# Second halves of the forgetting group's values and of the output weights moved behind the next step's minima

## The reference

```python
u = rmsnorm(h, g_attn)
qa, ka, va, logf, qb, kb, vb = project(u, w_in, b_forget)
oa = fox_prompt(qa, ka, va, logf)     # 8 heads x 64, causal, bias sum of log forget
ob = swa_prompt(qb, kb, vb, rel_bias, sinks)   # window of 3 chunks of 64, with sinks
...
# fox: s = q k^T * scale + (c_q - c_k); p = softmax(s); o = p v
# the rows ka, va, logf are outputs too (fox_k, fox_v, fox_logf)
mixed = concat([rmsnorm(oa, g_out_a), rmsnorm(ob, g_out_b)])
h = h + mixed @ w_out
u = rmsnorm(h, g_ffn)
h = h + (silu(u @ w_gate) * (u @ w_up)) @ w_down
y = rmsnorm(h, g_final)
```

## Time and profile before

| | |
|---|---|
| Median of 3 runs | 1428.67 us (1427.84 to 1430.19) |
| The profiled execution's own time | 1427.94 us |
| Its span in the profile | 1426.1 us |
| TensorE busy | 1387.8 us, 97% of the span |
| VectorE, ScalarE, GpSimd busy | 576.9, 481.4, 213.4 us |
| Forgetting steps | from about 216 to 560 us |

### The profile page before, as it was taken

How to read it: one execution, slowest core, us unless ns; L and a number is a source line. 1 busy time by engine, 2 the same in 40 slices (tenths; PEclk the granted TensorE clock), 3 DMA queues, 4 the chain that set the end, 5 groups by cost and what they waited for, 6 DMA issues and landing times.

```text
span 1426.1 us, 22599 instructions
## 1 busy us (share of the span) xinstructions
PE 1387.8 (97%) x9041; PEld 1287.2 (90%) x9041; DVE 576.9 (40%) x1378; ACT 481.4 (34%) x1049; POOL 213.4 (15%) x317
## 2 busy tenths in 40 slices
PE   6999999999999899999999999999999999999997
PEld 5989898788888677889999999999999999999997
DVE  6345634242323433662343424242525252525156
ACT  6346555655554652553212121212121111121103
POOL 3145551634443330000000000000000000000000
PEclk9999999999999899999999999999999999999999
DMA  7621124212120444314202020202020202020003
GB/s 199 116 69 38 32 73 158 84 43 80 52 82 16 149 163 150 106 45 123 74 16 75 15 74 16 74 15 75 16 74 16 74 20 72 26 76 16 16 1 122
DMA packets 110256, 97.64 MB, mean 68 GB/s; under 512 B 15937, under 2 KB 96929, under 8 KB 109641
## 3 DMA queue, kind: packets, MB, share of 16 engines
q1 hardware_dynamic: 110152, 96.20, 23.2%
HBM read 77.07 MB, written 19.21 MB: 68 GB/s over the span
## 4 chain that ended last, share of the span: by engine, by line
PE 90%; DVE 3%; DMA 3%; ACT 2%; issue 2%; POOL 1%; SPq 0%; ACTq 0%; DVEq 0%
PE ps L602 28%; PE ps L603 26%; PE ps L604 26%; PE ps L806 2%; PE ps L736 1%; PE ps L953 1%; DMA cb<-c_scratch 1%; DMA ob<-o_scratch 1%; PE ps L818 1%; PE ps L683 1%; DVE ps L1645 1%; PE ps L897 1%; PE ps L774 1%; ACT sp_x L1276 0%; PE ps L701 0%
## 5 line engine op out<-in xcount | busy, mean ns | idle before, releaser
L1892 DVE TENSOR_TENSOR outs<-outs,ps 128x384 f32<-128x384 f32 (+1 forms) x264 | 134.4, 509 | 108.1 <-PE ps L604 107.8
L1878 DVE TENSOR_TENSOR gu<-ps,sg 128x384 f32<-128x384 f32 (+1 forms) x66 | 34.6, 524 | 237.6 <-PE ps L604 237.6
L2062 POOL TENSOR_TENSOR pl_x<-sp_x,ph_x 128x512 fp32r<-128x512 f32 (+5 forms) x120 | 102.2, 865 | 168.0 <-ACT sp_x L1276 166.7
L1456 ACT ACTIVATE h_hi<-gu 128x384 fp32r<-128x384 f32 (+1 forms) x66 | 32.9, 498 | 222.2 <-DVE gu L1878 222.2
L1275 ACT ACTIVATE ph_x<-ps,negc 128x512 fp32r<-128x512 f32 (+5 forms) x120 | 62.9, 524 | 83.6 <-PE ps L818 83.6
L1450 ACT ACTIVATE sg<-ps 128x384 f32<-128x384 f32 (+1 forms) x66 | 30.4, 465 | 171.7 <-PE ps L604 171.7
L602 PE MATMUL ps<-f_hi,ff0hi 128*128 128x384 f32 (+1 forms) x264 | 85.7, 325 | 0.0
L602 PE MATMUL ps<-f_hi,ff1hi 128*128 128x384 f32 (+1 forms) x264 | 85.6, 324 | 0.0
L602 PE MATMUL ps<-f_hi,ff2hi 128*128 128x384 f32 (+1 forms) x264 | 85.6, 324 | 0.0
L602 PE MATMUL ps<-f_hi,ff3hi 128*128 128x384 f32 (+1 forms) x264 | 85.6, 324 | 0.0
L603 PE MATMUL ps<-f_lo,ff0hi 128*128 128x384 f32 (+1 forms) x264 | 85.3, 323 | 0.0
(11 more groups left out here) (311 smaller groups left out, 3770.8 us busy)
## 6 DMA issues: line engine op xcount, KB each, us to landing
raw<-in_w_gate SPq DMA_DIRECT2D x22, 512.0 KB, 4.7
raw<-in_w_up SPq DMA_DIRECT2D x22, 512.0 KB, 4.8
raw<-in_w_down SPq DMA_DIRECT2D x22, 512.0 KB, 3.9
raw<-in_w_in SPq DMA_DIRECT2D x14, 512.0 KB, 4.1
cb<-c_scratch SPq DMA_DIRECT2D x4, 1312.0 KB, 7.2
xt<-in_x_prompt SPq DMA_DIRECT2D x8, 512.0 KB, 4.2
out<-outb SPq DMA_DIRECT2D x16, 256.0 KB, 2.9
ob<-o_scratch SPq DMA_DIRECT2D x16, 256.0 KB, 3.1
```

The lines of the kernel that those rows point to most:

```text
L1456: act.activation(h_hi[par][:, f, c0:c0 + n], gu[(f + c) % 2][:, 0:n], ACT.Copy).then_inc(S["g_hi"], 1)
L1878: dve.tensor_tensor(gu[(f + c) % 2][:, 0:n], bank(3 + c, n), sg[c][:, 0:n], ALU.mult)\
L1892: add = dve.tensor_tensor(y, y, bank(b, whole * P).rearrange("p (t m) -> p t m", t=whole), ALU.add)
L2062: pool.tensor_tensor(pl_x[at][0:rows, 0:n], sp_x[at][0:rows, 0:n], ph_x[at][0:rows, 0:n].bitcast(F32), ALU.subtract).then_inc(S["x_pl"], 1)
```

## The change

Three things are moved; no instruction is added or left out.

1. On ScalarE the first halves `vw_hi` (L1222, L1221) leave the task. The copy to `outb` stays where it was; the first halves now stand behind `fox_exp` of the step after the copy (pieces in part 3) or of the same step (the piece in part 0).
2. On VectorE, for every v, the second halves `vw_lo` stand behind the minima of that step.
3. On VectorE the second halves of the output weights leave the end of step v and stand behind the minima of step v + 1.

New semaphores `v_hi` and `v_lo` count the values' halves; the store of the rows waits for the copy alone (`fv_out`).

```diff
@@ ScalarE
                     out.then_inc(S["fv_out"], 1)
-                    act.wait_ge(S["fv_out"], rows_out(n))
-                    if i >= 1:
-                        act.wait_ge(S["x_pv"], 2 * (NFU * (i - 1) + {0: 8, 4: 12, 8: NFU}[t0]))
...
-                    act.activation(vw_hi[0:m, t0:t0 + count, 0:3:2, :], kept.rearrange("p n (h d) -> p n h d", h=2),
-                                   ACT.Copy).then_inc(S["ev_act"], 1)
+            def values_hi(*place):
+
+                for item, a in plan(*place):
+                    if item == "task" and TASKS[a[0]][0] == "fv":
...
+                        rows = outb[STORES.index(n) % 2][0:m, 0:count, :]
+                        act.activation(vw_hi[0:m, t0:t0 + count, 0:3:2, :], rows.rearrange("p n (h d) -> p n h d", h=2),
+                                       ACT.Copy).then_inc(S["v_hi"], 1)
...
                 if 0 <= v < NX:
                     fox_exp(v)
+                values_hi("x", v - 1, 3)
+                values_hi("x", v, 0)
@@ VectorE
             for v in range(-LEAD, NX + 2):
-                if v < 0:
...
-                else:
-                    if v == 0:
-                        values_lo(-1, 3)
-                    for part in range(5):
-                        items("x", v, part)
+
+                if v >= 0:
+                    items("x", v, 0, but="fv")
+                items("x", v, 1)
+                out_weights_lo(v - 1)
+                values_lo(v - 1, 3)
+                values_lo(v, 0)
+                for part in (2, 3, 4):
+                    items("x", v, part, but="fv")
                 if v == ROOT_AT:
                     roots_b()
-                for k in range(KB):
-                    if OUT_AT[k] == v:
-                        dve.wait_ge(S["cw_hi"], SPLIT_OUT + k + 1)
...
@@ SyncE
-                sp_.wait_ge(S["ev_act"], act_done(n))
+                if kind == "fv":
+                    sp_.wait_ge(S["fv_out"], rows_out(n))
+                else:
+                    sp_.wait_ge(S["ev_act"], act_done(n))
```

More of the change, by code:

```diff
@@ L304 @@
 LAST_LEAD = max(_item[1] for _item, _banks in HELD if _banks[0] > 1)
[L306 to L307 removed]
+BY_ACT = ("sk", "ck", "sv", "bias", "amw", "amx", "fk", "fc", "tb")
+BY_DVE = ("ck", "sv", "negc", "otw", "otx", "fc", "tb")
 def act_done(n):
@@ L1160, in task @@
                 b = 4 + BANK_OF["task", n]
-                if kind not in BY_ACT:
+                if kind not in BY_ACT and kind != "fv":
                     return
@@ L1212, in task @@
                     out.then_inc(S["fv_out"], 1)
[L1213 to L1223 removed]
+            def values_hi(*place):
+                for item, a in plan(*place):
+                    if item == "task" and TASKS[a[0]][0] == "fv":
+                        n = a[0]
+                        i, t0, count = TASKS[n][1]
+                        m = rows_of(t0)
+                        if i >= 1:
+                            act.wait_ge(S["x_pv"], 2 * (NFU * (i - 1) + {0: 8, 4: 12, 8: NFU}[t0]))
+                        elif t0 == 0:
+                            act.wait_ge(S["w_pv"], 2 * NWU)
+                            act.wait_ge(S["w_ttr"], 4 * NWU)
+                        if t0 == 8:
+                            act.wait_ge(S["cv_in"], 16 * (i + 1))
+                            act.activation(vw_hi[:, 9:11, 0:3:2, :], cache_v[:].rearrange("p n (h d) -> p n h d", h=2), ACT.Copy)
+                        act.wait_ge(S["fv_out"], rows_out(n))
+                        rows = outb[STORES.index(n) % 2][0:m, 0:count, :]
+                        act.activation(vw_hi[0:m, t0:t0 + count, 0:3:2, :], rows.rearrange("p n (h d) -> p n h d", h=2),
+                                       ACT.Copy).then_inc(S["v_hi"], 1)
             def items(*place):
@@ L1581, in task @@
                                       rows.rearrange("p n (h d) -> p n h d", h=2),
-                                      hi[0:m, t0:t0 + count, 0:3:2, :].bitcast(F32), ALU.subtract).then_inc(S["ev_dve"], 1)
+                                      hi[0:m, t0:t0 + count, 0:3:2, :].bitcast(F32), ALU.subtract).then_inc(S["ev_dve" if kind == "sv" else "v_lo"], 1)
                 elif kind == "tb":
@@ L1706, in values_lo, with out_weights_lo @@
                         task(*a)
+            def out_weights_lo(v):
+                for k in range(KB):
+                    if OUT_AT[k] == v:
+                        dve.wait_ge(S["cw_hi"], SPLIT_OUT + k + 1)
+                        dve.scalar_tensor_tensor(out=wo_lo[:, k, :], in0=raw2d[k % 3], scalar=gw_col[:, OUT_K[k]:OUT_K[k] + 1],
+                                                 in1=wo_hi[:, k, :].bitcast(F32), op0=ALU.mult, op1=ALU.subtract)\
+                           .then_inc(S["cw_lo"], 1)
             def items(*place, but=None):
```

23 lines of the change are left out of this document (8 added, 15 removed).

## The result

The kernel with the change took 1438.61 us (median of 4 runs, 1435.29 to 1439.76), the kernel before, run beside it, 1428.79 us (4 runs, 1427.84 to 1430.19). The ratio is 1.0064 with an interval of [1.0050, 1.0077]: the change makes the kernel **slower**, by 9.8 us of medians. The forecast was 1436.4 us, within 1432.0 to 1440.0. The profiled execution of the change was its fastest, 1435.29 us (span 1433.5), which is 7.35 us over the profiled one of before.

What follows compares the result with a forecast made beforehand. TensorE, busy 1387.8 of 1426.1 us, was taken as the bound. The terms 5.5 + 2.6 - 0.4 = 7.7 us on the profiled 1427.94 gave 1435.6, against the median 1436.4 us, range 1432.0 to 1440.0.

Steps and rivals of the forecast that it cites:

- Points 1 and 2: Step 46: copy to `outb` and L774 0.54 us sooner (469.17); VectorE's minima first, L701 1.5 us sooner (471.28).
- Point 3: Step 46: division and `tb` queue behind the put-off halves on VectorE, so L695 starts 1.6 us later, at 475.28.
- Point 4: Step 47: first output projection step waits for four weights until 484.76, 5.5 us late in all, 3.9 from here.
- Point 5: Clock falls again behind step 47's new wait; 5.2 us of work run at half, 2.6 us lost.
- Point 6: Pairs 1 and 2: L701's 0.21 us waits at steps 16 and 31 go, 0.4 us won; pair 0: zero.
- the prediction's last sign of being wrong: The forecast is wrong if TensorE waits longer anywhere outside steps 45 to 48.
- Point 7: SyncE: output weights 3 and 4 are loaded 2.9 us later than now, which costs nothing.
- The sum: Whole kernel: 5.5 + 2.6 - 0.4 = 7.7 us lost on the profiled execution's 1427.94.
- A: No second fall of the clock, 1433.8, or clock full in step 46 too, 1430.4; chance 0.18.
- B: GpSimd's `pl_x` holds VectorE up 0.9 us in each of steps 46 and 47: 9.5 us lost, 1438.2; chance 0.15.
- C: TensorE free at L701 1.5 us sooner, nothing late next, clock full: 5.2 us won, 1423.5; chance 0.03.
- D: The late step is made up behind 485 us, by 1 to 5 us: 1431.4 to 1435.4; chance 0.04.

Runs made afterwards that it cites:

- e6: The change, with GpSimd's work of steps 46 and 47 held back until VectorE's `vw_lo` and `wo_lo` are done: 1437.28 us, ratio 1.0058.
- e4: The change, but output weights 0 and 1 split at the end of step 45 as before; only 2 and 3 behind step 47's minima: 1435.31 us, ratio 1.0043.
- a0: The change once more: 1438.82 us, ratio 1.0059; its D, the distance from step 45's minima matmuls to step 47's `tb`, 27.68 us.
- e5: The change, with 16 unused matmuls on TensorE ahead of the wait for the fourth `wo_lo`: 1436.75 us, ratio 1.0057.
- e7: Kernel before with values' halves moved as in the change, and output weight 0 one step sooner, in step 44: 1429.43 us, ratio 0.9999.
- e10: Kernel of e7 with unused matmuls (7, 6, 6) in TensorE's three waits of steps 45 and 46: 1428.70 us, ratio 0.9992.
- e9: Kernel before with only the values' halves moved, plus unused matmuls (5, 5, 6, 4) in TensorE's waits of steps 45 and 46: 1429.27 us, ratio 0.9997.
- e11: Kernel before, nothing moved, with unused matmuls (8, 5, 9) in TensorE's three waits of steps 45 and 46: 1430.18 us, ratio 1.0005.

## Why the prediction held, and where it was off

- **Points 1 and 2 held.** L774 of step 46 at 469.12 (said 469.17), L701 at 471.38 (471.28). The gain on ScalarE is 0.8 rather than 0.54 us when taken from L616, which is itself 0.22 us later; the trace starts `ot_x` 0.47 us after the large copy to `outb` (465.86), where the `vw_hi` of before began only 0.64 us after it.
- **Point 3 held in mechanism; the term was too small by 0.45 us.** L695 at 475.73 (said 475.28). The minima began 0.80 us behind L774, not 0.67, and from the start of the first `wo_lo` to that of `vw_lo` it was 2.95 us, not 2.40; the other terms were together 0.23 us shorter. Of the latter, e6 shows the cause: GpSimd's `pl_x` (to 471.94) beside the first `wo_lo`. L774 of step 47 came at 479.93, 0.33 before the forecast, because the clock rose at the same 478.9 as before, when less of the work had been done.
- **Point 4 held in mechanism, and its number by luck:** L602 at 484.93 (said 484.76), 5.70 us late. The two `wo_lo` took 3.00 us and not 2.48, for the same reason as in point 3, and the 0.33 us by which L774 came early made up for most of it. The wait before L602 (4.49 us, said 3.9) is the centre of the loss, and e4, where it is 4.48, shows that it belongs to weights 2 and 3 alone; 1.26 us of the 5.70 are there at L774 already.
- **Point 5 held in mechanism; its size was too large here, and varies:** 2.6 us said, 1.9 in the profiled execution and 2.4 in a0 (5.25 less 2.88). The prediction let 5.2 us run at half; it was 4.2 (484.93 to about 489.1). e5 takes the cost away by itself.
- **Point 6 is the step that failed.** It said −0.4 us for pairs 1 and 2. The two waits of 0.21 us before L701 are gone, but L774 one step on, which had no wait before, now waits for the division:

```profile
319.45 0.50 PE L774 MATMUL ps<-k_hi,q_hi 64*128 64x512 f32 x2 [0.23 <-DVE og_x L1640]
...
397.10 0.50 PE L774 MATMUL ps<-k_hi,q_hi 64*128 64x512 f32 x2 [0.22 <-DVE og_x L1640]
```

  So L701 of step 16 comes 0.36 us sooner (315.56), but the next L774 only 0.04 (319.45 after 319.49), and that of step 32 comes 0.10 later (397.10 after 397.00). Instead of 0.4 us ahead, the change is 0.23 us behind when step 45 begins; no single wait accounts for the rest of the difference. The division stands behind the pieces of `vw_lo`, as worked out in point 3 for the last pair. I had not carried the same queue over to the others. One of these pieces also ran beside `pl_x` and took 1.12 us instead of 0.69, for the reason of e6:

```profile
316.36 1.12 DVE L1593 TENSOR_TENSOR vw_lo<-outb,vw_hi 128x512 fp32r<-128x512 f32 x1 [0.97 <-ACT vw_hi L1231]
```

  For pair 0 zero was said. Its L774 of step -3 came 0.42 us later (237.15 after 236.73) and the next only 0.03 (240.84 after 240.81), where the wait shrank from 0.97 to 0.57 us. So it was. But the prediction's last sign of being wrong, a longer wait of TensorE outside steps 45 to 48, came true three times: here (0.91 us after 0.41) and at the two L774 above. For pairs 1 and 2 it was wrong; the loss that was forecast does not rest on them.
- **Point 7 held:** ScalarE went through both weights 2 and 3 without an idle stretch, so the later loads cost nothing.
- **The sum** was 7.7 us on the profiled execution, and 7.35 came. That it is so near is in part luck: 0.7 us too much for the clock (point 5) and 0.6 too much won before step 45 (point 6) cancel. Against the medians it was too small by 1.3 to 2.1 us (9.0 and 9.8). The traces account for 1.3 of it: a0's D is +8.65, in the slowest of its runs, where the profiled execution, the fastest of its, has +7.38, and nearly all of the difference lies in how long the clock stayed low. What is left is inside the intervals.
- **The rivals.** A fell: the clock went down twice. B was partly true: GpSimd's reading does hold VectorE up, but by 0.55 and 0.52 us, not by 0.9 each time. Its 1438.2 is nearer to the measured 1438.61 than the forecast's 1436.4, but its mechanism gave only 1.07 of the 1.8 us that it asked for. The sum "by that rule", up to 9.7 us in the prediction, would be 9.5 with B's 0.9 us taken twice. C fell by its own test, the room of 0.89 and 0.56 us. D fell: 7.61 us late at `tb` of step 47, 7.4 at the end of the span.

For the term of point 3 the trace now settles what the earlier trace rows left open. One `wo_lo` that began while `pl_x` was reading took 1.83 us (first row, the change); alone it took 1.28 (second row, e7):

```profile
471.19 1.83 DVE L1726 SCALAR_TENSOR_TENSOR wo_lo<-raw,small,wo_hi 128x1024 fp32r<-128x1024 f32 x1
```

```profile
469.99 1.28 DVE L1726 SCALAR_TENSOR_TENSOR wo_lo<-raw,small,wo_hi 128x1024 fp32r<-128x1024 f32 x1 [2.78 <-ACT wo_hi L1101]
```

That is 0.55 us for an overlap of 0.75 (471.19 to 471.94). The Trainium skill's page "SBUF — State Buffer", section "Who interferes with whom", says that a VectorE instruction with two inputs in SBUF and a GpSimd instruction that reads SBUF contend, and that the order of issue decides who is blocked. By that rule the trace agrees, in both directions: `wo_lo` behind `pl_x`, the cast behind `wo_lo` (1.20 us, alone 0.20).

No version here beats the kernel before beyond doubt. The nearest is e10, 0.9992 [0.9983, 1.0001].

## What to carry to other kernels

Work that is put off behind an engine's urgent instruction lands ahead of that engine's next urgent one, so compare it with the slack there, at every place where the pattern repeats: here 3.6 us of halves against 0.89, and 4.5 us (minima and two weights) against 0.56. An engine that stands idle before the urgent instruction, with the input of the later work there already, is a sign that its order, not its load, is at fault. A low clock is a cost only as far as no other chain of the same length runs beside it: look at who else starts from the same instruction before you count its microseconds as to be won.

## What the runs showed of the hardware that was not expected

- TensorE's clock fell although TensorE had stood for only short times. In the change it fell at about 468.7, some 0.9 us into the wait of 1.32 us before L774 (469.12), with one wait of 1.30 us (before L616 at 465.08) ahead of it and 2.7 us of work between. With matmuls in these waits, as in e9 and e11, the same stretch kept 1.00. The moment varies: in e6, with the same work and waits up to L701 (1.31, 1.33 and 1.47 us), the clock was 1.00 in the stage 468 to 472 and 0.63 in the next.
- Nor did filling always hold it: e10 lost the clock at 480, just behind a wait of 1.69 us, with 19 unused matmuls put in. Waits of 1.70 and 1.68 us at the same place in e9 and e11 left it at 1.00.
- The lengthening of a VectorE instruction beside a reading GpSimd (0.55 us) is less than their overlap (0.75 us). Why 0.2 us are missing no run here tells.
